# Hybrid RWKV-7 and attention trunk in float32: halves of U copied by two engines, splits placed earlier, norm rows fetched block by block, 48 instead of 40 steps in a layer's last pair

## The reference

```
y_r, v_r = rwkv7_mix(z_rwkv, v_first, vres, ...)      # a state of 64x64 per head, updated per token
y_a = moba_attention(rope(q), rope(k), v)             # softmax over the causal keys
y = concatenate([y_r, y_a]) @ w_out
x = x + rms_norm(y, norm_mix_post)
h = rms_norm(x, norm_mlp_pre)
m = square(relu(h @ w_up)) @ w_down
x = x + rms_norm(m, norm_mlp_post)
```

## Time and profile before

| | us |
|---|---|
| median of 3 runs | 2487.6 |
| lowest, highest | 2487.11, 2488.59 |
| the profiled execution | 2488.29 |
| its span, first to last instruction | 2486.4 |
| TensorE busy | 2455.4 |
| VectorE busy | 1681.4 |
| ScalarE busy | 1252.2 |
| GpSimd busy | 129.6 |

### The profile page before, as it was taken

The page is one execution under the profiler, slowest core; times in us unless marked ns, Lnnn a source line. Parts: engine busy times, 40 slices in busy tenths (PEclk is TensorE's granted clock), DMA queues, the critical chain, the costliest instruction groups (busy, mean ns, idle before and its releaser), DMA issues.

```text
span 2486.4 us, 47886 instructions
## 1 busy us (share of the span) xinstructions
PE 2455.4 (99%) x15931; PEld 2060.0 (83%) x15931; DVE 1681.4 (68%) x2809; ACT 1252.2 (50%) x2048; POOL 129.6 (5%) x186
## 2 busy tenths in 40 slices
PE   8999999999999999999999999999999999999998
PEld 7888888788888888888788888877888888888887
DVE  6778877576566566466578888885765565664665
ACT  6555655464344344344455565555553443443443
POOL 3000100000000000000011111100000000000000
PEclk9999999999999999999999999999999999999999
DMA  7444444655656555665554444445556656566564
GB/s 211 138 121 120 138 135 125 196 184 187 195 182 194 193 183 193 195 186 187 160 147 126 128 120 135 126 126 199 182 179 201 183 190 194 178 196 193 184 194 152
DMA packets 437963, 420.06 MB, mean 169 GB/s; under 512 B 19566, under 2 KB 352000, under 8 KB 437888
## 3 DMA queue, kind: packets, MB, share of 16 engines
q1 hardware_dynamic: 434240, 412.55, 53.4%
q0 software_dynamic: 3648, 6.52, 0.9%
HBM read 416.90 MB, written 2.10 MB: 169 GB/s over the span
## 4 chain that ended last, share of the span: by engine, by line
PE 97%; DVE 1%; ACT 1%; DMA 1%; issue 0%; SPq 0%; POOL 0%; DVEq 0%; POOLq 0%
PE gemm_bank L538 33%; PE gemm_bank L539 18%; PE gemm_bank L565 11%; PE gemm_bank L566 11%; PE gemm_bank L567 11%; PE gemm_bank L541 2%; PE mix_banks L718 1%; PE mix_banks L725 1%; PE mix_banks L689 1%; PE mix_banks L760 1%; PE mix_banks L766 1%; PE mix_banks L765 1%; PE mix_banks L756 1%; PE mix_banks L590 0%; PE mix_banks L661 0%; PE mix_banks L659 0%
## 5 line engine op out<-in xcount | busy, mean ns | idle before, releaser
L1228 DVE TENSOR_TENSOR b_wlo<-b_raw,b_whi 128x1024 fp32r<-128x1024 f32 x777 | 944.7, 1225 | 533.0 <-ACT b_whi L923 531.9
L538 PE MATMUL gemm_bank<-b_hT,b_whi 128*128 128x512 f32 x3420 | 1248.5, 405 | 1.7 <-DVE b_hT L1280 1.1
L923 ACT ACTIVATE b_whi<-b_raw 128x1024 fp32r<-128x1024 f32 x777 | 810.3, 1056 | 624.0 <-PE gemm_bank L567 414.2
L539 PE MATMUL gemm_bank<-b_hT,b_wlo 128*128 128x256 f32 x3648 | 1011.7, 281 | 0.0
L538 PEld LDWEIGHTS gemm_bank<-b_hT,b_whi 128*128 128x128 f32 x3420 | 643.3, 188 | 154.6 <-issue 7.3
L539 PEld LDWEIGHTS gemm_bank<-b_hT,b_wlo 128*128 128x128 f32 x3648 | 689.7, 189 | 9.8
L565 PE MATMUL gemm_bank<-b_whi,b_mT 128*128 128x512 f32 x1280 | 501.4, 392 | 0.7 <-DVE b_wlo L1228 0.7
L567 PE MATMUL gemm_bank<-b_whi,b_mT 128*128 128x512 f32 x1280 | 498.3, 389 | 0.0
L566 PE MATMUL gemm_bank<-b_wlo,b_mT 128*128 128x512 f32 x1280 | 498.3, 389 | 0.0
L565 PEld LDWEIGHTS gemm_bank<-b_whi,b_mT 128*128 128x128 f32 x1280 | 240.4, 188 | 50.3 <-ACT b_whi L923 1.1
L567 PEld LDWEIGHTS gemm_bank<-b_whi,b_mT 128*128 128x128 f32 x1280 | 240.3, 188 | 50.0
(11 more groups left out here) (234 smaller groups left out, 1776.3 us busy)
## 6 DMA issues: line engine op xcount, KB each, us to landing
b_raw<-in_w_up SPq DMA_DIRECT2D x256, 512.0 KB
b_raw<-in_w_down SPq DMA_DIRECT2D x256, 512.0 KB
b_raw<-in_w_in SPq DMA_DIRECT2D x384, 256.0 KB
b_raw<-in_w_out SPq DMA_DIRECT2D x60, 512.0 KB
b_raw<-in_w_in SPq DMA_DIRECT2D x8, 512.0 KB
b_xt<-in_x SPq DMA_DIRECT2D x8, 256.0 KB, 5.3
b_raw<-in_w_out SPq DMA_DIRECT2D x8, 256.0 KB
out<-b_xt SPq DMA_DIRECT2D x8, 256.0 KB, 2.4
```

Of the source, the lines that this page charges most:

```text
L538: mm(bank[b0 + b][:, :], whi[r][:, cols], pair, start=first, stop=False)
L539: m = mm(bank[b0 + b][:, 0:SEQ], wlo[r][:, cols], act[:, kt, 0, :], start=False, stop=False)
L923: f(whi[r][:, :], raw[r][:, :, :].rearrange("p a b -> p (a b)"), ACT.Copy).then_inc(hi_done, 1)
L1228: tt(wlo[r][:, :], flat(raw[r][:, :, :]), whi[r][:, :].bitcast(F32), ALU.subtract).then_inc(lo_done, 1)
```

## The change

It does five things.

- U's two blocks are copied by two engines: ScalarE copies the first (rows 0 to 63), VectorE the second (`second_u`), in each of the four chunks of all 16 mixers.
- `step(2)` is called before the gram masks on VectorE and before the copies of v and kb on ScalarE, and each later step one place on, so that the steps reach 7 in the chunks. On VectorE step 5 before chunk 0 and step 6 in chunk 1 become step 6 in chunk 0; step 7 comes in chunk 3 ahead of y's sum (L1520).
- Mask and maxima move from chunk 2 to chunk 1, the exponentials to chunk 1, the key shifts and the reciprocal of the sums to chunk 2, the scaling of the probabilities to chunk 3, ahead of the key square.
- In a layer's last pair the limit is 48 instead of 40: the eight half steps of slots 6 and 7 are handed out in the mixer, with `fill(3)` more ahead of the wait for `y_norm`. Steps 7 and 8 of that pair come in chunks 2 and 3 on VectorE, step 8 in chunk 1 on ScalarE.
- The gain rows have a semaphore each and other buffers (qr, sh, VU, xs). GpSimd fetches rows 0 and 1 when the scores are summed, row 2 after y's sum, row 3 after yn. VectorE waits for a block's own row.

```diff
-        gain_row = [xs..., qr..., sh[:, 1:3, :]..., VU...]
+        gain_row = [qr..., sh[:, 1:3, :]..., VU..., xs...]
-        gain_row_in = sem("gain_row_in")
+        gain_row_in = [sem(f"gain_row_in_block{i}") for i in range(NB)]
...
-                pool.wait_ge(e["o_lo"], PAIRS * (l + 1))
-                pool.wait_ge(e["pair_done"], PAIRS * (l + 1) + 1)
-                fetch_gain_row(2 * l, norm_mix_post[l])
+                n = PAIRS * (l + 1)
+                pool.wait_ge(e["turned"], n)
+                pool.wait_ge(e["bonus_ready"], n)
+                pool.wait_ge(e["scaled"], 4 * n)
+                pool.wait_ge(e["score_sum"], n)
+                if l == 0:
+                    pool.wait_ge(e["v_kept"], n)
+                fetch_gain_row(0, norm_mix_post[l])
+                fetch_gain_row(1, norm_mix_post[l])
+                pool.wait_ge(e["y_sum"], n)
+                fetch_gain_row(2, norm_mix_post[l])
+                pool.wait_ge(e["y_sq"], n)
+                pool.wait_ge(e["y_norm"], 4 * n)
+                fetch_gain_row(3, norm_mix_post[l])
+                pool.wait_ge(e["o_lo"], n)
+                pool.wait_ge(e["pair_done"], n + 1)
...
 TensorE, mixer
+                if not more:
+                    fill(3)
                 pe.wait_ge(e["y_norm"], 4 * n + 4)
...
-                    lambda a, b: last_ticks(a, b, k + 92, t + 46), 40), False)
+                    lambda a, b: last_ticks(a, b, k + 92, t + 46), 48), False)
...
 ScalarE, mixer
                     act.wait_ge(e["u_sum"], NCH * n + c + 1)
-                    for h in range(2):
-                        hs = slice(HEAD * h, HEAD * h + HEAD)
-                        f(VU[opp(c), c, hs], mb[3][hs, ...], ACT.Copy).then_inc(e["u_out"], 1)
+                    f(VU[opp(c), c, 0:HEAD], mb[3][0:HEAD, 256:320], ACT.Copy).then_inc(e["u_out"], 1)
...
 VectorE, mixer
-                step(5)
                 dve.wait_ge(e["akv_out"], V)
                 dve.wait_ge(e["e_chunk"], V)
+                def second_u(c):
+                    dve.wait_ge(e["u_sum"], NCH * n + c + 1)
+                    nc.vector.tensor_copy(VU[opp(c), c, HEAD:P], mb[3][HEAD:P, 320:384]).then_inc(e["u_out"], 1)
                 for c in range(NCH):
                     if c:
                         dve.wait_ge(e["r_sum"], (NCH - 1) * n + c)
                         tt(Rb[...], mb[0][...], AKV[...], ALU.add).then_inc(e["r_out"], 1)
+                    if c == 0:
+                        second_u(c)
+                        step(6)
                     if c and c < NCH - 1:
                         ts(Sc, St[:, c - 1, :], eC[:, c:c + 1], None, ALU.mult).then_inc(e["s_old"], 1)
                     if c == 1:
-                        step(6)
-                    if c == 2:
                         dve.wait_ge(e["score_sum"], V)
                         tt(sm[:, :], mb[2][:, 0:384], ..., ALU.add).then_inc(e["masked"], 1)
+                        second_u(c)
                         dve.wait_ge(e["masked"], V)
...
+                    if c == 2:
+                        second_u(c)
+                        if more:
+                            key_shift(l, i + 1, n + 1, 0)
...
-                    if c == 2 and more:
-                        key_shift(l, i + 1, n + 1, 0)
-                    if c == 3 and more:
-                        key_shift(l, i + 1, n + 1, 1)
-                        key_square(l, i + 1, n + 1)
+                    if c == 2:
+                        dve.wait_ge(e["expd"], 2 * n + 2)
+                        nc.vector.reciprocal(small[:, 14:16], small[:, 12:14]).then_inc(e["rsum"], 1)
+                        if more:
+                            key_shift(l, i + 1, n + 1, 1)
+                        else:
+                            step(7)
+                    if c == 3:
+                        second_u(c)
+                        dve.wait_ge(e["rsum"], V)
+                        ts(sm[:, 0:P], ...)
+                        ts(sm[:, P:3 * P], ...).then_inc(e["probs"], 1)
+                        if more:
+                            key_square(l, i + 1, n + 1)
+                        step(7 if more else 8)
                 dve.wait_ge(e["y_sum"], V)
...
-                step(7)
...
-                    if nb == 0:
-                        dve.wait_ge(gain_row_in, 64 * (2 * l + 1))
+                    dve.wait_ge(gain_row_in[nb], 32 * l + 16)
```

More of the change, by code:

```diff
@@ L487, in unit, with fetch_gain_row @@
                     nc.gpsimd.tensor_copy(vf[:, bass.ds(i, 1), :], sh[:, 2:3, :]).then_inc(e["v_kept"], 1)
[L489 to L493, removed]
+            def fetch_gain_row(nb, gain):
+                pool.dma_start(gain_row[nb], gain[block_cols(nb)].unsqueeze(0).to_broadcast([P, 512]))\
+                    .then_inc(gain_row_in[nb], 16)
             for l in range(DEPTH):
@@ L509, in _ @@
                      lambda: pair_weights(l + 1, 0) if l < DEPTH - 1 else None)
[L511 to L513 removed]
+                n = PAIRS * (l + 1)
[14 more added lines that the diff above has]
+                pool.wait_ge(e["pair_done"], n + 1)
                 pool.wait_ge(x_new, 8 * (2 * l + 1))
                 nc.gpsimd.memset(yof, 0.0).then_inc(clears, 1)
[L516 removed]
+                for nb in range(NB):
+                    fetch_gain_row(nb, norm_mlp_post[l])
         @block.tensor
@@ L634, in last_ticks @@
                     s, j, u = (x - KT) // 4, (x - KT) % 4 // 2, x % 2
-                    half_tick(k + KT // SK + s, 0, j, u, OUT_SLOTS[s][1 + j], 0, x < KT + 2, False)
+                    nb = OUT_SLOTS[s][0]
+                    first = s in (0, 7) and j == 0
+                    if first and nb and u == 0:
+                        pe.wait_ge(tile_out, tiles + 2)
+                    half_tick(k + KT // SK + s, 0, j, u, OUT_SLOTS[s][1 + j], 2 * nb, first, False)
             pe.wait_ge(first_in, 16)
@@ L849, in _ @@
                     first = s == [w[0] for w in OUT_SLOTS].index(nb)
-                    if s < 6:
+                    if s < 8:
                         continue
-                    if first and nb == 1:
-                        pe.wait_ge(tile_out, t)
-                    elif first:
+                    if first:
                         pe.wait_ge(y_out, 40 * l + 2 * nb - 2)
@@ L1040, in mixer @@
                 step(1)
+                step(2)
                 act.wait_ge(e["turned"], V)
@@ L1045, in mixer @@
                 f(kbT[:, :, :].rearrange("p a b -> p (a b)"), bank[1][:, 0:3 * P], ACT.Copy).then_inc(e["kb_out"], 1)
-                step(2)
                 step(3)
+                step(4)
                 for lv in range(1, LEVELS):
@@ L1053, in mixer @@
                     if lv == 2:
-                        step(4)
+                        step(5)
                     if lv == 3:
@@ L1089, in mixer @@
                               accum_out=small[:, 12 + a:13 + a]).then_inc(e["expd"], 1)
+                        if not more:
+                            step(8)
                     if c == 3:
@@ L1105, in attention_hi @@
                       ACT.Copy).then_inc(e["o_hi"], 1)
-                if not more:
+                if more:
+                    step(8)
+                else:
                     attention_hi()
-                step(8)
                 step(9)
@@ L1431, in mixer @@
                 merge(0, 1, mb[3][:, 0:P]).then_inc(e["z_ready"], 1)
-                step(2)
+                step(3)
                 for lv in range(1, LEVELS):
@@ L1439, in mixer @@
                     if lv == 2:
-                        step(3)
+                        step(4)
                     if lv == 3:
@@ L1504, in mixer @@
                         finish(1)
-                    if c == 2 and more:
-                        key_shift(l, i + 1, n + 1, 0)
-                    if c == 3 and more:
-                        key_shift(l, i + 1, n + 1, 1)
-                        key_square(l, i + 1, n + 1)
[L1511 to L1515, removed]
+                    if c == 2:
[3 more added lines that the diff above has]
+                            key_shift(l, i + 1, n + 1, 1)
+                        else:
+                            step(7)
+                    if c == 3:
+                        second_u(c)
+                        dve.wait_ge(e["rsum"], V)
+                        ts(sm[:, 0:P], sm[:, 0:P], small[:, 14:15], None, ALU.mult)
+                        ts(sm[:, P:3 * P], sm[:, P:3 * P], small[:, 15:16], None, ALU.mult).then_inc(e["probs"], 1)
+                        if more:
+                            key_square(l, i + 1, n + 1)
+                        step(7 if more else 8)
                 dve.wait_ge(e["y_sum"], V)
```

12 lines of the change are left out of this document (3 added, 9 removed).

## The result

| | before | after |
|---|---|---|
| median, us | 2488.64 (14 runs, 2486.01 to 2491.72) | 2494.97 (14 runs, 2492.85 to 2496.91) |
| ratio, with its 95% interval | | 1.0026 (1.0018 to 1.0034) |
| from one loop pair to the next, layer 0 | 49.83 | 50.47 |
| the same, layer 1 | 50.64 | 51.19 |
| last pair and output projection, layer 0 and layer 1 | 116.51, 116.22 | 114.79, 115.54 |

The account below looks back on a forecast made before the run. TensorE, 99% busy, was taken to bound the kernel, with ScalarE and VectorE in step in the mixers' chunks. Loop pairs +4.2, last pairs -0.8 each, gain rows -0.8 made +1.8 us: 2489.3 us, range 2484.0 to 2495.0.

Parts of the forecast that it names:

- my own case: L796 (L814 after) in the 14 loop pairs: waits for late yn, +0.30 us a pair, +4.2 in all; chance 0.63.
- the slower rival: L796 in loop pairs: chunk 0's losses not won back, last U sum 0.45 later, 0.75 a pair, 2495.7 us; chance 0.17.
- The faster rival: VectorE keeps pace, St of chunk 0 and yn in time: 0.71 us saved each loop pair, 2475 us; chance 0.1.
- the term of chunk 0: VectorE's copy (0.28), split (1.22), then St (0.60), joints 0.08 before the end: St at TensorE +0.28 us.
- Chunks 1 to 3: U gains 0.11 us in each, chunk 3's L756 some 0.15; with chunk 0, -0.20 at the last product.
- The gains of U: Two-engine U copy in the chunks: U about 0.18 us earlier, late weight load gone, 0.11 at each of four chunks.
- The tail: Loop pair behind chunk 3: key square late, +0.14; tick's wait gone, -0.27; yn late at L796; +0.30 us a pair.
- The last pairs and the gain rows: Half steps: net -0.8 us in each last pair; gain rows by block: -0.8 in layer 0, nothing in layer 1.
- the rival by which the half steps do nothing: Last pairs: eight half steps gain 0, as slot 8's split or the pair's end binds; +3.4, 2491.0 us; chance 0.1.
- the gain rows' 0.8: Layer 0, L565: its 0.74 us idle behind VectorE's late gain rows goes, forecast as -0.8 us.
- within 0.2%: Whole kernel: median not told apart from no change, about 5 us either way; chance 0.73.
- each of five joints: Loop pair: 0.05 us either way allowed in each; with both ends of the copy, -0.13 to +0.55 a pair.

Follow-up runs that it names:

- The experiments with step 7 and the key square: Two runs on the changed kernel, loop pairs: step 7's split behind y's sum again, 2490.01 us; key square ahead of chunk 3's U copy, 2490.95 us.
- the run with the old fetch and without the stall: Kernel before with only the loop pairs' ScalarE and VectorE code changed, last pairs and gain rows as before: 2496.36 us, ratio 1.0030.
- the rows alone: Kernel before with only the gain rows fetched earlier, block by block: one run of 2489.15 us.
- the version with all three moves: Changed kernel with chunk 0's U copied by ScalarE alone, step 7 behind y's sum, key square ahead of U's copy: 2478.61 us; halves exchanged too, 2477.18.

## Why the prediction was wrong

**What bounds, and the yn wait.** Right. TensorE does the same work; L814 waits for yn in just the 14 loop pairs, the place of my own case and of the slower rival. That rival named chunk 3's U sum 0.45 later than my own case and 0.75 a pair; measured are 0.35 (+0.24 for my -0.11) and 0.64 and 0.55 a pair, 2494.97 beside its 2495.7. Its place and price were nearly right, and it had a chance of only 0.17. But the reason that it gave, a copy on VectorE that comes later than ScalarE's second did, is not what happened: in chunk 1 the copy ended at 392.36, where ScalarE's two copies of 0.46, begun at 392.07, would have ended at 392.53. So the nearness of its number is partly luck. The faster rival, VectorE keeping pace, falls with chunk 0's St: the loads no longer wait for U and the kernel is slower all the same.

**The step that failed** is the term of chunk 0, "a following VectorE instruction starts 0.08 before the end of the one before", and its +0.28. Measured is +0.47. The copy took 0.23, not 0.28 (0.05 for me); but its two joints, copy to split and split to St, were at +0.03 instead of -0.08, 0.22 against me. I had read -0.08 in rows where both neighbours use the same partitions, and applied it to new neighbours that do not. The same rows showed the other value too: L1520, whose second half works in partitions 64 to 127, ends at 395.18, and the split behind it starts at 395.21. The load of L772 waited 0.8 us a time (13.1 in 16), where I had named 0.5.

**Chunks 1 to 3.** "St there is ready when its sum is, nothing lost" was wrong by 0.08: St of chunk 1 stands behind the copy and both maxima, with two joints at +0.03, mask to copy and L1513 to St (+0.37 to +0.45). The gains of U were as forecast, 0.10 in chunk 1 and 0.10 in chunk 2, and the state of chunk 2 comes 0.11 earlier for 0.15 forecast. Sum at the last product: +0.12 in place of -0.20. This difference of 0.32 carries most of the miss of a pair, and over 14 pairs (0.34 and 0.25 each) the pairs carry 4.1 us of it.

**The tail.** The waits came where I put them: the load of L662 0.27 late on the key square (0.25 forecast, 394.25 for 394.00), the tick behind it free, L1554 behind a split, and yn 0.05 ahead of L814. The experiments with step 7 and the key square took 0.43 and 0.36 out at these two places. At y's sum I had again counted -0.08 behind the split, and it was +0.03. So yn came 0.39 later than I had it: 0.35 from U's sum of chunk 3 (+0.24 for -0.11), 0.11 from this joint, less 0.05 for the shorter copy and 0.02 elsewhere; TensorE took it up 0.05 faster than I had reckoned, which makes +0.64 in place of +0.30.

**The last pairs and the gain rows.** -0.8 twice and -0.8 in layer 0 were forecast, -2.4 in sum; measured are -1.72 and -0.68, -2.4. Waits at L792 and L796 are gone. Rb of chunk 3 stands behind a split, and TensorE's product from it comes 1.64 us behind the state's (447.35 to 448.99), where it was 1.02 (441.33 to 442.35): +0.6, as costed. That the sum is the -2.4 I forecast is in part chance. Layer 0's -1.72 is against an execution with the stall at L565; against the run with the old fetch and without the stall (115.49) it is -0.70, beside layer 1's -0.68. So a last pair gives 0.7, for 0.8 forecast, and the rival by which the half steps do nothing falls by layer 1, where the rows alone gave nothing (+0.16). That the gain rows' 0.8 belongs to the stall at L565 is not shown, since that stall failed to appear in a run with the old fetch.

**The sum and the range.** 2489.3 forecast, 2494.97 measured, just inside the high end of 2495.0. I forecast "within 0.2%" at 0.73, and +0.26% came. A term repeated 14 times was known to 0.05 us in each of five joints; that is 3.5 us if they all err one way. Those that did err had one cause and erred by 0.11 each, twice what I allowed.

## What to carry to other kernels

When TensorE and a helper engine are in step to a tenth of a microsecond, a split of 1.2 us put between a copy and the instruction that frees TensorE is paid in full, and nearly all of the lateness reaches the end of the stage: move such work to where that engine waits for another's answer anyway (behind y's sum, while ScalarE squares). When costing a new order of small VectorE instructions, take each joint from a row with the same partitions on both sides; here a change of start partition cost 0.11 us, and the choice of which half an engine copies was worth 0.36 us a pair in the changed kernel and 0.08 in the version with all three moves.

## What the runs showed of the hardware

In the rows read here VectorE's joints have two values, about 0.08 us ahead of the recorded end and 0.03 behind it, and exchanging the copied halves moved St and y's sum from the second to the first.

The granted clock fell to half behind a pause of TensorE, in some executions only. The pause was the same each time: idle for 1.55 us, eight small matmuls (L588, L600), idle for 0.57. Why it brings the lower clock in one execution and not in another is not shown. At the start of layer 0's MLP the changed kernel's row of busy time by stretch (stretch, us, busy us of PE, PEld, DVE, ACT and POOL, clock, DMA share, GB/s) reads:

```profile
528.72:531.40 2.68, 2.68 (x8) 2.29 (x9) 2.68 (x5) 2.68 (x9) 0.00 (x0) 0.50 0.00 0
```

Before had full clock there, but 0.61 at the same place in layer 1:

```profile
524.70:527.30 2.60, 2.60 (x15) 2.27 (x16) 2.60 (x5) 2.60 (x9) 0.00 (x0) 1.00 0.00 0
1764.90:1767.50 2.60, 2.58 (x9) 2.23 (x10) 2.60 (x5) 2.60 (x8) 0.00 (x0) 0.61 0.03 6
```

From ScalarE's first L958 (L974) behind layer 0's output projection to the one behind its MLP took 711.7 us in the profiled execution of before and 713.1 in that of after; the other profiled executions, of both kernels' variants, lie within 0.2 us of one or the other. Such a step of 1.4 us in the time of an execution is twice what a last pair gained.
